# A gMLP's value half: weights that stay, transposes behind the gelu, and a row norm finished on GpSimd

## The reference, cut to what matters

```python
def gmlp_mixer(h, w_in, ln_g, ln_b, w_s, b_s, w_out):
    u, v = jnp.split(jax.nn.gelu(h @ w_in, approximate=False), 2, axis=-1)
    v = layer_norm(v, ln_g, ln_b)
    vg = v.reshape(B, T // tc, tc, GM_GROUPS, GM_GROUP_DIM)      # tc = 128 or 4
    ws = w_s[:, :tc, :tc] * jnp.tril(jnp.ones((tc, tc), w_s.dtype))
    mixed = jnp.einsum('gij,bcjgd->bcigd', ws, vg) + b_s[:, :tc].T[None, None, :, :, None]
    return (u * mixed.reshape(B, T, GM_WIDTH)) @ w_out, v
```

## Time and profile before

| | |
|---|---|
| median of 3 runs | 1644.56 us (1643.82 to 1647.26) |
| the profiled execution | 1642.12 us, its span 1640.4 us |
| PE busy | 1594.5 us, 97% of the span |
| DVE busy | 1257.1 us, 77% |
| ACT busy | 993.0 us, 61% |
| POOL busy | 54.6 us, 3% |
| granted TensorE clock, mean | 0.984 |

### The profile page before, as it was taken

How to read it: one execution, slowest core, us unless ns; L and a number is a source line. 1 busy time by engine, 2 the same in 40 slices (tenths; PEclk the granted TensorE clock), 3 DMA queues, 4 the chain that set the end, 5 groups by cost and what they waited for, 6 DMA issues and landing times.

```text
span 1640.4 us, 22161 instructions
## 1 busy us (share of the span) xinstructions
PE 1594.5 (97%) x8419; PEld 1359.7 (83%) x8419; DVE 1257.1 (77%) x1220; ACT 993.0 (61%) x951; POOL 54.6 (3%) x62
## 2 busy tenths in 40 slices
PE   7998989999999997999999999999999999999998
PEld 5886978999998885888888888888888888888886
DVE  4487453666544848988988988988988988988986
ACT  3442452444444446777777777767777777777774
POOL 3430000000000000000000000000000000000000
PEclk9999989999999998999999999999999999999999
DMA  7274445324556424999999999999999999999970
GB/s 231 82 304 148 173 155 205 143 89 167 205 194 206 157 97 153 366 347 359 358 347 357 356 350 358 361 344 357 355 356 355 361 356 343 368 354 337 370 276 29
DMA packets 194262, 444.15 MB, mean 271 GB/s; under 512 B 10840, under 2 KB 13946, under 8 KB 194202
## 3 DMA queue, kind: packets, MB, share of 16 engines
q1 hardware_dynamic: 190082, 436.91, 73.3%
q10 hardware_dynamic: 4120, 6.42, 1.1%
HBM read 439.57 MB, written 3.74 MB: 270 GB/s over the span
## 4 chain that ended last, share of the span: by engine, by line
PE 91%; DVE 6%; issue 1%; ACT 1%; ACTq 0%; DMA 0%; DVEq 0%
PE bank L1718 20%; PE bank L2125 13%; PE bank L2127 12%; PE bank L2126 12%; PE bank L2135 6%; PE bank L2137 6%; PE bank L2136 6%; PE bank L1710 3%; PE bank L1889 2%; PE bank L2143 1%; PE bank L2098 1%; DVE rt L1312 1%; DVE ring_r L1172 1%; PE bank L2113 1%; PE bank L2114 1%
## 5 line engine op out<-in xcount | busy, mean ns | idle before, releaser
L1553 DVE TENSOR_TENSOR wql<-ring,wqh 128x2048 fp32r<-128x2048 f32 x336 | 767.9, 2290 | 112.3 <-ACT wqh L760 109.1
L760 ACT ACTIVATE wqh<-ring 128x2048 fp32r<-128x2048 f32 x336 | 646.4, 1925 | 260.5 <-PE bank L2127 171.9
L2125 PE MATMUL bank<-wqh,xgh 128*128 128x512 f32 x896 | 357.6, 399 | 4.1 <-DVE wql L1553 2.5
L2127 PE MATMUL bank<-wqh,xgl 128*128 128x512 f32 x896 | 350.7, 391 | 0.0
L2126 PE MATMUL bank<-wql,xgh 128*128 128x512 f32 x896 | 350.0, 391 | 0.0
L2125 PEld LDWEIGHTS bank<-wqh,xgh 128*128 128x128 f32 x896 | 169.1, 189 | 38.6 <-DVE wql L1553 3.3
L2127 PEld LDWEIGHTS bank<-wqh,xgl 128*128 128x128 f32 x896 | 168.8, 188 | 36.5
L2126 PEld LDWEIGHTS bank<-wql,xgh 128*128 128x128 f32 x896 | 169.3, 189 | 33.2
L2135 PE MATMUL bank<-wqh,heTh 128*128 128x512 f32 x448 | 174.9, 390 | 1.9 <-DVE heTl L1553 1.9
L2137 PE MATMUL bank<-wqh,heTl 128*128 128x512 f32 x448 | 175.0, 391 | 0.0
L2136 PE MATMUL bank<-wql,heTh 128*128 128x512 f32 x448 | 175.0, 391 | 0.0
(11 more groups left out here) (353 smaller groups left out, 2075.5 us busy)
## 6 DMA issues: line engine op xcount, KB each, us to landing
ring<-in_moe_w_gate SPq DMA_DIRECT2D x56, 2048.0 KB, 8.3
ring<-in_moe_w_up SPq DMA_DIRECT2D x56, 2048.0 KB, 8.4
ring<-in_moe_w_down SPq DMA_DIRECT2D x56, 2048.0 KB, 8.4
ring<-in_attn_w_in SPq DMA_DIRECT2D x7, 2048.0 KB, 10.2
ring<-in_ffn_w_gate SPq DMA_DIRECT2D x5, 2048.0 KB, 8.7
ring<-in_ffn_w_up SPq DMA_DIRECT2D x5, 2048.0 KB, 7.7
ring<-in_cache_k SPq DMA_DIRECT2D x16, 512.0 KB, 12.8
ring<-in_cache_v SPq DMA_DIRECT2D x16, 512.0 KB, 5.6
```

Source lines behind the costliest of these rows:

```text
L760: return nc.scalar.activation(dst, src, ACT.Copy)
L1553: return v.tensor_tensor(dst, src, head.bitcast(F32), ALU.subtract)
L2125: mm(bank, xgh[:, k, :], w_h[:, part], start=(k == 0), stop=False)
L2127: last = mm(bank, xgl[:, k, :], w_h[:, part], start=False, stop=(k == KD - 1))
```

## The change

The value half is projected like the gate half: 8 groups `("gv", c)` with the weights stationary and 288 tokens moving, from column quarters in place of row quarters. The first three groups run in two passes (chunks 0 to 3, then 4 to 7), with the wait for the tails of x at each chunk; the sum of squares follows them. VectorE multiplies each group by rt into the new tile `gvT` (features on partitions), ScalarE applies the gelu in place. `rk` and its products are gone. Behind the first gate group TensorE turns gvT to rows in six groups `("gvt", m, half)`; ScalarE copies the first half of each row block into gv, VectorE the second. The statistics (`row_stats`) follow behind gate group 0, the roots behind group 1, subtract and scale (`row_scale`, not linked to each other) behind group 2. The product with ln_g and the sum with ln_b are GpSimd's, for each row block behind `ln_scaled`, with a wait after each instruction. The declarations of gvT and of the semaphores are left out below.

```diff
...
@@ -389,5 +391,4 @@
     B.add(("ssq", 2), "act")
-    for half in range(2):
-        for m in range(3):
-            A.add(("gv", m, half), "act")
+    for c in range(KD):
+        A.add(("gv", c), "dve")
     for q in range(2):
@@ -396,2 +397,6 @@
         A.add(("gu", c), "dve")
+        if c == 0:
+            for m in range(3):
+                for half in range(2):
+                    A.add(("gvt", m, half), ("act", "dve")[half])
         if c == 1:
@@ -443,3 +448,3 @@
             stream += [(("fd", half, part), over)]
-    stream += [(("gv", i), A.full(("gv", 2, i))) for i in range(2)]
+    stream += [(("gv", i), A.full(("gv", 4 * i + 3))) for i in range(2)]
     stream += [(("gu", i), A.full(("gu", 4 * i + 3))) for i in range(2)]
@@ -468,4 +473,3 @@
             quarters += [(("fd", half, part), "rows", q) for q in range(min(8, NFB - 8 * part) // 2)]
-    for half in range(2):
-        quarters += [(("gv", half), "rows", q) for q in range(QU)]
+    quarters += [(("gv", c // 4), "cols", c % 4) for c in range(KD)]
     quarters += [(("gu", c // 4), "cols", c % 4) for c in range(KD)]
@@ -736,3 +740,12 @@
         pool.wait_ge(*A.freed(("wst", 1)))
-        select(wsT[:], ALU.is_ge, 0.0, 0, [[0, 8], [1, P]], -1).then_inc(ws_ok, 1)
+        ins = select(wsT[:], ALU.is_ge, 0.0, 0, [[0, 8], [1, P]], -1)
+        ins.then_inc(ws_ok, 1)
+        pool.wait_ge(ws_ok, 1)
+        pool.wait_ge(gm_in, 48)
+        for m in range(3):
+            r = ROWS[m]
+            pool.wait_ge(ln_scaled, m + 1)
+            link(nc.gpsimd.tensor_tensor(gv[0:r, m, :], gv[0:r, m, :], lng[0:r, :], ALU.mult))
+            nc.gpsimd.tensor_tensor(gv[0:r, m, :], gv[0:r, m, :], lnb[0:r, :], ALU.add).then_inc(ln_ok, 1)
+            pool.wait_ge(ln_ok, m + 2)
 
@@ -1001,17 +1014,9 @@
                       a["gm_b_s"].rearrange("o g i -> o (g i)").broadcast_to([P, 8 * P])).then_inc(gm_in, 16)
-        heads_before(GV0 + QU + WD - 1)
+        heads_before(GV0 + WD + 2)
         act.wait_ge(*B.full(("ssq", 2)))
-        sums = B.ap(("ssq", 2))
-        nc.scalar.activation(rk[:, 0:2], sums[:, T:T + 2 * E:E], ACT.Sqrt, bias=epst[:, 0:1], scale=1.0 / D)
-        nc.scalar.activation(rk[0:NS, 2:3], sums[0:NS, T + 2 * E:T + 2 * E + 1], ACT.Sqrt, bias=epst[0:NS, 0:1],
-                             scale=1.0 / D)
-        nc.scalar.activation(rt[:], sums[:, 0:T], ACT.Sqrt, bias=epst[:, 0:1], scale=1.0 / D).then_inc(b_act, 1)
-        for half in range(2):
-            heads_before(GV0 + QU * half + QU + WD)
-            for m in range(3):
-                act.wait_ge(*A.full(("gv", m, half)))
-                act.wait_ge(rk_ok, 1)
-                r = ROWS[m]
-                nc.scalar.activation(gv[0:r, m, CH * half:CH * half + CH], A.ap(("gv", m, half))[0:r, :], ACT.Gelu,
-                                     scale=rk[0:r, m:m + 1]).then_inc(a_act, 1)
+        nc.scalar.activation(rt[:], B.ap(("ssq", 2))[:, 0:T], ACT.Sqrt, bias=epst[:, 0:1], scale=1.0 / D).then_inc(b_act, 1)
+        for c in range(KD):
+            heads_before(GV0 + c + 1 + WD)
+            act.wait_ge(*A.freed(("gv", c)))
+            nc.scalar.activation(gvT[:, c, :], gvT[:, c, :], ACT.Gelu).then_inc(gvT_ok, 1)
         for q in range(2):
@@ -1019,5 +1024,2 @@
             copy(wsT[:, 4 * q:4 * q + 4, :], A.ap(("wst", q))[:].rearrange("p (g i) -> p g i", g=4)).then_inc(a_act, 1)
-        act.wait_ge(ln_ok, 1)
-        nc.scalar.activation(mv[:, 0:2, 2:3], mv[:, 0:2, 1:2], ACT.Sqrt, bias=epst[:, 0:1])
-        nc.scalar.activation(mv[0:NS, 2, 2:3], mv[0:NS, 2, 1:2], ACT.Sqrt, bias=epst[0:NS, 0:1]).then_inc(lnroot, 1)
         for c in range(KD):
@@ -1026,2 +1028,10 @@
             nc.scalar.activation(gu[:, c, :], gu[:, c, :], ACT.Gelu).then_inc(gelu_ok, 1)
+            if c == 0:
+                for m in range(3):
+                    act.wait_ge(*A.full(("gvt", m, 0)))
+                    copy(gv[0:ROWS[m], m, 0:CH], A.ap(("gvt", m, 0))[0:ROWS[m], :]).then_inc(a_act, 1)
+            if c == 1:
+                act.wait_ge(ln_ok, 1)
+                nc.scalar.activation(mv[:, 0:2, 2:3], mv[:, 0:2, 1:2], ACT.Sqrt, bias=epst[:, 0:1])
+                nc.scalar.activation(mv[0:NS, 2, 2:3], mv[0:NS, 2, 1:2], ACT.Sqrt, bias=epst[0:NS, 0:1]).then_inc(lnroot, 1)
         act.wait_ge(ln_ok, 4)
@@ -1452,6 +1462,4 @@
                 tails_before(GV0 + WD - 1)
-        tails_before(GV0 + QU + WD - 1)
+        tails_before(GV0 + WD + 2)
         dve.wait_ge(*B.freed(("ssq", 2)))
-        v.reciprocal(rk[:, 0:2], rk[:, 0:2])
-        v.reciprocal(rk[0:NS, 2:3], rk[0:NS, 2:3]).then_inc(rk_ok, 1)
         v.reciprocal(rt[:], rt[:]).then_inc(r_ok, 1)
@@ -1462,13 +1470,32 @@
 
-        tails_before(GU0 + WD)
-        for m in range(3):
-            r = ROWS[m]
-            for half in range(2):
-                dve.wait_ge(*A.freed(("gv", m, half)))
-                v.bn_stats(bn[0:r, m, 6 * half:6 * half + 6], gv[0:r, m, CH * half:CH * half + CH]).then_inc(ln_bad, 1)
-            dve.wait_ge(ln_bad, 2 * m + 2)
-            ins = v.bn_aggr(mv[0:r, m, 0:2], bn[0:r, m, :])
-        ins.then_inc(ln_ok, 1)
+        for c in range(KD):
+            dve.wait_ge(*A.full(("gv", c)))
+            v.tensor_tensor(gvT[:, c, :], A.ap(("gv", c))[:, 0:T], rt[:], ALU.mult).then_inc(a_dve, 1)
+            tails_before(GV0 + c + 1 + WD)
+
+        def row_stats():
 
-        def row_norm():
+            for m in range(3):
+                r = ROWS[m]
+                dve.wait_ge(*A.full(("gvt", m, 1)))
+                v.tensor_copy(gv[0:r, m, CH:D], A.ap(("gvt", m, 1))[0:r, :]).then_inc(a_dve, 1)
+                for half in range(2):
+                    dve.wait_ge(*A.freed(("gvt", m, half)))
+                    v.bn_stats(bn[0:r, m, 6 * half:6 * half + 6], gv[0:r, m, CH * half:CH * half + CH]).then_inc(ln_bad, 1)
+                dve.wait_ge(ln_bad, 2 * m + 2)
+                ins = v.bn_aggr(mv[0:r, m, 0:2], bn[0:r, m, :])
+            ins.then_inc(ln_ok, 1)
+
+        def mix_of_samples():
+
+            dve.wait_ge(*A.full("wsr"))
+            v.tensor_copy(wst4[:], A.ap("wsr")[0:NS, 0:8 * TS].rearrange("p (g i) -> p g i", g=8)).then_inc(a_dve, 1)
+            dve.wait_ge(*A.freed("wsr"))
+            for g in range(8):
+                last = v.tensor_tensor(wsS[:, g, :].rearrange("p (b i) -> p b i", i=TS),
+                                       wst4[:, g, :].unsqueeze(1).broadcast_to([NS, NSEQ, TS]),
+                                       bmask[:].unsqueeze(2).broadcast_to([NS, NSEQ, TS]), ALU.mult)
+            last.then_inc(wsS_ok, 1)
+
+        def row_scale():
 
@@ -1477,14 +1504,7 @@
             link(v.reciprocal(mv[0:NS, 2, 3:4], mv[0:NS, 2, 2:3]))
-            dve.wait_ge(gm_in, 48)
             for m in range(3):
                 r = ROWS[m]
-                link(v.tensor_scalar(gv[0:r, m, :], gv[0:r, m, :], mv[0:r, m, 0:1], mv[0:r, m, 3:4],
-                                     ALU.subtract, ALU.mult))
-                yield
-                link(v.tensor_tensor(gv[0:r, m, :], gv[0:r, m, :], lng[0:r, :], ALU.mult))
-                yield
-                v.tensor_tensor(gv[0:r, m, :], gv[0:r, m, :], lnb[0:r, :], ALU.add).then_inc(ln_ok, 1)
-                yield
+                v.tensor_scalar(gv[0:r, m, :], gv[0:r, m, :], mv[0:r, m, 0:1], mv[0:r, m, 3:4],
+                                ALU.subtract, ALU.mult).then_inc(ln_scaled, 1)
 
-        norming = row_norm()
         for c in range(KD):
@@ -1493,16 +1513,8 @@
             tails_before(GU0 + c + 1 + WD)
+            if c == 0:
+                row_stats()
+            if c == 2:
+                row_scale()
             if c == 1:
-                dve.wait_ge(*A.full("wsr"))
-                v.tensor_copy(wst4[:], A.ap("wsr")[0:NS, 0:8 * TS].rearrange("p (g i) -> p g i", g=8)).then_inc(a_dve, 1)
-                dve.wait_ge(*A.freed("wsr"))
-                for g in range(8):
-                    last = v.tensor_tensor(wsS[:, g, :].rearrange("p (b i) -> p b i", i=TS),
-                                           wst4[:, g, :].unsqueeze(1).broadcast_to([NS, NSEQ, TS]),
-                                           bmask[:].unsqueeze(2).broadcast_to([NS, NSEQ, TS]), ALU.mult)
-                last.then_inc(wsS_ok, 1)
-            else:
-                for _ in range(1 if c == 0 else 2):
-                    next(norming, None)
-        for _ in norming:
-            pass
+                mix_of_samples()
 
@@ -1696,7 +1708,2 @@
             last = mm(bank[:, 0:T], ones[:], rt[:], start=True, stop=True)
-            if n == 2:
-                for m in range(3):
-                    r = ROWS[m]
-                    last = mm(bank[0:r, T + E * m:T + E * m + E], rt[:, P * m:P * m + r], ones[:, 0:E],
-                              start=True, stop=True)
             last.then_inc(b_full, 1)
@@ -2026,6 +2033,19 @@
 
-        for half in range(2):
```

(30 more changed lines are left out.)

## The result

The changed kernel takes 1660.6 us in the median of 12 runs (1652.3 to 1667.0), the kernel before 1643.8 (1640.8 to 1651.9). The ratio of the runs is 1.009, 95% interval 1.0067 to 1.0114, so slower by 0.9%; the two medians by themselves are 16.8 us or 1.0% apart. The forecast was slower, by 6 us, 1650.3 in a range of 1642.0 to 1654.0; the loss is nearly three times the forecast one. The profiled execution took 1663.05 us, its span 1661.3.

The account below looks back on a forecast made before the run. Bound: the row norm's last add and VectorE's backlog before the mix. Later mix 4.8 plus slow clock 1.2 gave +6.0 us: 1648.1 on the profiled execution, 1650.6 on the median, stated as 1650.3; range 1642.0 to 1654.0.

Parts of the forecast that it names:

- The projection and the stall: Value half on TensorE: 8.6 us gained, less a 2.6 us third-quarter stall and 2.4 of transposes; TensorE 3.3 us earlier.
- The chain to the first scaling: VectorE and ScalarE work beside the gate groups: first scaling at 552.0, GpSimd's first rows at 552.8 us.
- GpSimd's price and the two-way lock: Row norm: six GpSimd instructions, 14.5 us, plus nearly all of VectorE's 7.6 by mutual blocking; mix later by 4.8 us.
- The clock: Mix after TensorE's idle wait: half clock for none to three groups, 0 to 2.3 us, taken as 1.2.
- The first (no hold-up): Rival, gate stage: GpSimd and VectorE hardly block each other, only VectorE's backlog goes; -2.0 us, 1642.6; chance 0.23.
- The third: Rival, gate stage: GpSimd always wins, VectorE's tails wait and TensorE's gate groups end late; +8 to +10, 1653.6; chance 0.09.

Follow-up runs that it names:

- e7: e1 with the value half's first pass over two groups instead of three and five small loads issued by SyncE instead of ScalarE; 1644.7 us, ratio 1.0003.
- e1: Changed kernel with the ln_g and ln_b steps back on VectorE between gate groups, new projection kept; 1650.1 us, ratio 1.0039 to the kernel before.
- e3: Changed kernel with 60 extra products on TensorE in front of its wait for the row norm; 1649.8 us, ratio 1.0025 to the kernel before.
- e4: Changed kernel with the last five weight tails of the stage replaced by a memset to zero, which reads nothing; 1651.7 us in one run.
- e2: Kernel before, old projection, with ln_g and ln_b on GpSimd and subtract and scale behind gate group 0; 1652.1 us, ratio 1.0025.
- e8: e7 with all copies to rows on ScalarE and the norm fused to two VectorE instructions per row block; 1642.7 us, ratio 0.9992.
- e11: e8 with two steps of the norm behind each gate group instead of one; 1636.3 us, ratio 0.9949 to the kernel before.
- e9: Kernel before with six extra 128x1024 copies on VectorE in front of the norm's last add; 1653.1 us, ratio 1.0049.
- e12: e8 with 24 extra products on TensorE in front of its wait for the norm; 1643.6 us, ratio 0.9989.
- e10: e9 with 28 extra products on TensorE in front of its wait for the mix; 1651.4 us, ratio 1.0044.

## Why the prediction was wrong

- **The projection and the stall: right.** Predicted was a stall of 2.6 us at the third quarter, measured 2.50. The last gate group was to end 3.3 us earlier than before, or, held up by the tails, 59.7 to 62.0 us behind the start; it ended at 60.9, 0.6 earlier than before. So the sum came out, but by other parts. The tails held TensorE for 0.4 us and not for 1 to 3. Of the 2.7 us between 3.3 and 0.6, some 1.5 are the 3.3 us at half the clock that the stall set off, which the prediction did not have, 0.4 that tail; the rest, under a microsecond over the whole walk, I have not placed. e7, where the mix starts 4.4 us earlier than in e1, shows that the stall was on the path.
- **The chain to the first scaling: right.** Predicted 552.0 - 505.1 = 46.9 us behind the start, measured 562.02 - 513.91 = 48.1; the 1.2 are about that slow stretch.
- **GpSimd's price and the two-way lock: right.** I took 14.5 us and nearly all of VectorE's 7.6; measured 20.3. The last add was to end 68.4 to 69.6 us behind the value half's start; it ended at 69.4. The chain began 1.4 us later than predicted and was 1.0 shorter than its middle value (20.3 for 21.3), so part of the hit is luck. With the clock held up (e3) the region is 5.5 us longer than before, where I had put 4.8.
- **The clock: the term that failed.** I wrote "None to three slow groups: 0 to 2.3 us; I take 1.2". All eight groups of the mix were slow, VectorE's starts 1.72 us apart in place of 1.30, and so was the beginning of the output projection. Measured 6.5 us (e3). The price of one slow group was not too low, 0.65 us foreseen and some 0.45 measured; their number was, and the output projection was left out: counted from the mix's start, the changed kernel is 4.0 us behind e3 at the eighth group's bias and 6.7 at the end of the output projection. The row I went by showed the clock at 0.50 for one window of 5 us in the attention stage and I took its length from there; that trace has it low from about 169.8 to 176.4 us. Here it was low for 23 us, from 578 to 601, 18 of them with TensorE at work. Why it stayed low that long no run isolates: in the mix TensorE waited for nobody, VectorE waited for it (0.33 us in each group), and the clock came back in the output projection.
- **The rivals.** The first (no hold-up) is out by the 3.0 us tails and by e4. The third's mechanism shows in e2, not here, where GpSimd and the tails took turns. What the prediction did not have among its rivals is that the first half of the change alone loses 6 us (e1). There the norm on VectorE ends 1.6 us later than before, TensorE waits for it, and the clock falls behind that wait too. Without the stall (e7) the same half loses nothing, 105.0 us: the stall and the slow stretch behind it are as large as those 6. The prediction priced a low clock only behind a wait for GpSimd.
- **The rest of the median,** 4.8 us, is most likely no step of the prediction but the spread of the starts: the spread of the attention stage was in the runs shown only as 1643.8 to 1647.3, and I had given 0.6 us for it. Even without it the forecast missed: 12.0 us on the median of before is 1655.8, outside the range. Why 8 of the 12 runs drew 1658 and more, and what sets that draw, stays open; no experiment was aimed at it.

## What to carry to other kernels

Making TensorE faster in front of a wait that another engine sets does not shorten the path, and the longer wait can slow what follows: here no clock was lost behind a wait of 0.9 us, and behind ones of 3.5, 5.3 and 8.6 us it cost 4.7, 4.6 and 6.5 more. First pull the other engine's work forward (its place in the list of instructions decided, e8 against e11), then speed up TensorE; where the wait can't go, spare products in it keep the clock. An elementwise step moved to GpSimd beside a busy VectorE is paid twice, in GpSimd's chain (20.3 us here, 15.4 with the tails taken away) and in the VectorE instructions from SBUF that meet it: tails of 1.22 us took 3.0, a scaling of 0.81 took 2.9, small ones of 0.17 up to 2.3.

## What the runs showed of the hardware

- After waits of TensorE of 3.52, 3.85, 5.28 and 8.58 us the clock was at 1.2 GHz for all or nearly all of the mix (e8, e1 and e7, e9, changed); after 0.9 us, and after the waits of 3.5, 5.3 and 8.6 filled with products (e12, e10, e3), at 2.4. Even 2.50 us (the stall) was followed by 3.3 us at 1.2 GHz.
- Work alone did not bring the clock back at once: TensorE was busy 13.84 of 13.84 us in the mix, at 0.50 throughout, and for 4 us more of the output projection.
- GpSimd's two-input instruction over 1024 elements costs the same on 32 partitions as on 128 (2.33 and 2.40 us in e4).
- Two traces of one kernel can be 10 us apart in a stage that no edit touches (the changed kernel's value half at 504.1 and 513.9), and agree to 0.1 us in the stage under study: for an edit of a few microseconds the regions of the traces say more than the medians.
